# Modulation sums of a two-block transformer: when GpSimd sums over the partitions, and where the down products take their modulation units

## What is computed

```python
def mod_vectors(cvec, w_mod, b_mod):
    m = jax.nn.silu(cvec) @ w_mod + b_mod
    return jnp.split(m, N_MOD, axis=-1)

def sandwich_ffn(x, w_gate_up, w_down, g_pre, g_post, shift, scale, gate):
    h = modulate(rms_norm(x, g_pre), shift, scale)
    return x + 0.5 * gate * rms_norm(swiglu(h, w_gate_up, w_down), g_post)

for l in range(DEPTH):                       # DEPTH 2, N_MOD 9
    mx = [m[:, None, :] for m in mod_vectors(c, w_mod[l], b_mod[l])]
    mc = mod_vectors(c_ctx, w_mod[l], b_mod[l])
    ...
    x = sandwich_ffn(x, w_ffn_gate_up[l, 0], w_ffn_down[l, 0], g[0], g[1], mx[0], mx[1], mx[2])
    ctx = sandwich_ffn(ctx, w_ffn_gate_up[l, 0], w_ffn_down[l, 0], g[0], g[1], mc[0], mc[1], mc[2])
    ...
```

## Time and profile before

| | us |
|---|---|
| median of 3 runs | 2505.74 (2501.82 to 2506.13) |
| the profiled run | 2505.95 |
| its span, first to last instruction | 2504.1 |
| TensorE busy in it | 2429.5 (97%), 12978 matmuls |
| VectorE busy | 1545.5 (62%) |
| ScalarE busy | 1017.6 (41%) |
| GpSimd busy | 335.9 (13%) |

### The profile page before, as it was taken

How to read it: one execution, slowest core, us unless ns; L and a number is a source line. 1 busy time by engine, 2 the same in 40 slices (tenths; PEclk the granted TensorE clock), 3 DMA queues, 4 the chain that set the end, 5 groups by cost and what they waited for, 6 DMA issues and landing times.

```text
span 2504.1 us, 30960 instructions
## 1 busy us (share of the span) xinstructions
PE 2429.5 (97%) x12978; PEld 2056.5 (82%) x12978; DVE 1545.5 (62%) x2102; ACT 1017.6 (41%) x1429; POOL 335.9 (13%) x226
## 2 busy tenths in 40 slices
PE   7999999999999999999999999999999999999998
PEld 4887778857888778888888769987888899887997
DVE  6878796364778797444375565455466545586544
ACT  4221325375312225322225464345555434465443
POOL 0334242200143252101020200000000000000000
PEclk8999999989999999999999989999999999999999
DMA  7565552511465553444362625555534455533553
GB/s 283 184 170 183 171 177 93 156 35 65 154 185 173 165 181 121 152 137 153 115 219 76 147 68 189 180 179 178 184 119 152 135 186 185 160 129 117 190 182 142
DMA packets 242491, 386.04 MB, mean 154 GB/s; under 512 B 10864, under 2 KB 150256, under 8 KB 242288
## 3 DMA queue, kind: packets, MB, share of 16 engines
q1 hardware_dynamic: 236176, 372.43, 45.3%
q0 software_dynamic: 6176, 11.64, 2.5%
HBM read 382.83 MB, written 3.11 MB: 154 GB/s over the span
## 4 chain that ended last, share of the span: by engine, by line
PE 65%; DVE 17%; DMA 10%; ACT 4%; issue 3%; POOL 1%; SPq 0%; DVEq 0%; ACTq 0%; POOLq 0%
PE ps L532 20%; PE ps L533 20%; PE ps L534 20%; DVE arena L1871 8%; DMA raw<-in_w_mod 6%; DVE wlo L1848 4%; ACT whi L1231 2%; DVE arena L1868 2%; PE ps L602 1%; DMA raw<-in_w_ffn_down 1%; DMA arena<-rpbs 1%; PE ps L853 1%; DMA arena<-in_w_mod 1%; DMA raw<-in_w_ffn_gate_up 1%; DMA grow<-gcol 1%
## 5 line engine op out<-in xcount | busy, mean ns | idle before, releaser
L1848 DVE TENSOR_TENSOR wlo<-raw,whi 128x2048 fp32r<-128x2048 f32 x279 | 668.5, 2397 | 552.2 <-ACT whi L1231 551.9
L1231 ACT ACTIVATE whi<-raw 128x2048 fp32r<-128x2048 f32 x279 | 532.9, 1910 | 1131.3 <-PE ps L534 679.3
L532 PE MATMUL ps<-wlo,Hhi 128*128 128x512 f32 (+1 forms) x1888 | 707.9, 375 | 17.1 <-DVE Hlo L2057 10.8
L534 PE MATMUL ps<-whi,Hhi 128*128 128x512 f32 (+1 forms) x1888 | 697.5, 369 | 0.0
L533 PE MATMUL ps<-whi,Hlo 128*128 128x512 f32 (+1 forms) x1888 | 697.2, 369 | 0.0
L532 PE MATMUL ps<-Hlo,whi 128*128 128x512 f32 (+1 forms) x1896 | 639.7, 337 | 4.4 <-DVE wlo L1848 4.4
L533 PE MATMUL ps<-Hhi,wlo 128*128 128x512 f32 (+1 forms) x1896 | 638.6, 337 | 0.0
L534 PE MATMUL ps<-Hhi,whi 128*128 128x512 f32 (+1 forms) x1896 | 638.6, 337 | 0.0
L532 PEld LDWEIGHTS ps<-wlo,Hhi 128*128 128x128 f32 x1888 | 358.3, 190 | 85.0 <-DVE Hlo L2057 13.3
L534 PEld LDWEIGHTS ps<-whi,Hhi 128*128 128x128 f32 x1888 | 358.1, 190 | 60.1
L533 PEld LDWEIGHTS ps<-whi,Hlo 128*128 128x128 f32 x1888 | 358.6, 190 | 56.5
(11 more groups left out here) (262 smaller groups left out, 1584.3 us busy)
## 6 DMA issues: line engine op xcount, KB each, us to landing
raw<-in_w_ffn_gate_up SPq DMA_DIRECT2D x88, 1024.0 KB, 5.2
raw<-in_w_mod SPq DMA_DIRECT2D x65, 1024.0 KB, 5.1
raw<-in_w_ffn_down SPq DMA_DIRECT2D x44, 1024.0 KB, 4.9
raw<-in_ffn_w_in SPq DMA_DIRECT2D x44, 1024.0 KB, 5.0
raw<-in_attn_w_in SPq DMA_DIRECT2D x36, 1024.0 KB, 5.1
raw<-in_ffn_w_out SPq DMA_DIRECT2D x22, 1024.0 KB, 4.9
raw<-in_w_in SPq DMA_DIRECT2D x16, 1024.0 KB, 5.0
raw<-in_mlstm_w_in SPq DMA_DIRECT2D x12, 1024.0 KB, 5.1
```

What stands on the lines that cost most here:

```text
L532: e.matmul(o, L[0], R[1], start=start, stop=False)
L534: return e.matmul(o, L[0], R[0], start=False, stop=stop)
L1231: e.activation(hi_of(n), slot(n), ACT.Copy).then_inc(*A.up(("hi", n)))
L1848: e.tensor_tensor(lo_of(n), slot(n), hi_of(n).bitcast(F32), ALU.subtract).then_inc(*V.up(("lo", n)))
```

## The change

Three things change.

1. GpSimd waits for more before a sum. For a half (l, v, h) with stream s it used to wait for the half's own last multiply-add ("side") alone. Now, unless the half is the last of a group (`GROUP_ENDS`, h = 1), it waits for ("sum", next half, 4 s, 0) too: stream 0 for VectorE's first product of the next half, stream 1 for the first multiply-add of the next half's second unit. The semaphore is the same one, with a higher value.
2. A half is taken four ticks after its last unit, no longer three.
3. `SIDE_DOWN_AT` is range(8), no longer range(2, 8): the eight modulation units of a down net stand one behind each of its weight units 0 to 7. Before, units 2 and 5 had two behind them, and 3, 4, 6 and 7 one.

```diff
@@ Feed.tick
-        if self.summed and self.ticks - self.summed[0][1] >= 3:
+        if self.summed and self.ticks - self.summed[0][1] >= 4:
             yield from self.one()
@@
-SIDE_AT, SIDE_DOWN_AT = range(2, NF // 2 - 1), range(2, NF // 2 - 3)
+SIDE_AT, SIDE_DOWN_AT = range(2, NF // 2 - 1), range(NF // 2 - 3)
+GROUP_ENDS = [g[-1] for g in [*SIDE.values(), *SIDE_DOWN.values()]]
@@ summed_over_partitions
                     w.wait_ge(*V.at(("side", l, v, h)))
                     for s in range(ns):
+                        if (l, v) not in GROUP_ENDS or h == 0:
+                            w.wait_ge(*V.at(("sum", *acc_prev[q + 1], 4 * s, 0)))
                         t = SUMS[q % RING][s]
                         e.partition_all_reduce(t, t, 128, bass.bass_isa.ReduceOp.add).then_inc(
```

## The result

The changed kernel took 2519.31 us (median of 4 runs, 2518.57 to 2519.69) beside 2505.22 us before: a ratio of 1.0056, interval 1.004 to 1.0072, or +14 us. The prediction said 2511 us with a range to 2518. The direction was the likelier of its two by a hair, the size was nearly three times too small, and the time lies 1.3 us above the range.

What follows compares the result with a forecast made beforehand. TensorE, busy 2429.5 of 2504.1 us, bounds the kernel, with 18.9 us of pauses to win. Terms of +2.1 and +1.8 us, plus 1 us for thin margin, on 2505.95 gave 2511 us; range 2490 to 2518.

Steps and rivals of the forecast that it cites:

- The wait for the columns: VectorE's wait for pcol at a taking: stays about as it is, zero, bound 2 us per vector half.
- The clock: TensorE's granted clock behind new pauses: no loss in the forecast sum, falls of 1.7 us each only in a rival.
- the slot: Raw's slot for modulation units in gate_up: 24.5 us per pair, against 24.1 before and 21.76 needed by TensorE.
- The hold: VectorE inside the modulation unit: each sum holds up one multiply-add by 2.0 us, making it 2.7 us.
- The two rivals by which sums would wait or slip: Sums beside multiply-adds: all wait, 2489 or 2497 us, chance 0.22; one gets in, one waits, 2498 us, chance 0.13.
- the burst of small DMAs for the first gate vector: In the first gate_up: comes one step later, as its taking does, and costs the same.
- its own sign for this: VectorE's waits for pcol over 2 us per taking would break the term put at zero.
- the 5.4 foretold: First gate_up: TensorE goes on 5.4 us later, behind the wlo after the last two sums.
- the walk: VectorE's new order followed from 90 us with forecast durations: the first gate_up's last modulation unit ends at 270.3 us.
- L2107: Pause at the first down product, behind a modulation unit ahead of the last multiplies: 4.7 for 0.9 us, +3.8, twice.
- The Hlo waits: TensorE's waits in both downs: go with one unit per step, nearly all won, -7.1 and -7.2 us.
- The rival that held the clock: Pauses in the gate_ups bring four to six clock falls, 7 to 10 us: 2518 to 2521 us; shares chance 0.12.

Runs made afterwards that it cites:

- e7: The changed kernel with a threshold of five ticks in place of four: 2517.71 us, ratio 1.0058 against the kernel before.
- e5: The kernel before with parts 2 and 3, and the last multiplies of gate_up ahead of the modulation unit: 2484.56 us, ratio 0.9928.
- e1: The kernel before with only part 3, the spread of the down units: 2500.15 us, ratio 0.9989.
- T, D, W: On the kernel before, threshold of four (T), then spread of down units (D), then GpSimd's new waits (W): ratios 0.9964, 0.9962, 1.0056.
- e6: The changed kernel with the old places of the down units, so parts 1 and 2: 2528.33 us, ratio 1.0101 against the kernel before.
- Part 2 alone: The kernel before with only the threshold raised from three to four ticks: 2491.98 us, ratio 0.9964.
- e9: The changed kernel with the new wait on a half's first sum only, the second right behind it: 2514.40 us, ratio 1.0032 against the kernel before.
- e4: The kernel before with parts 2 and 3, without GpSimd's new waits: 2491.07 us, ratio 0.9962.
- e2: The kernel before with only GpSimd's new waits, threshold still three: 2614.15 us, ratio 1.0449.
- e11: The changed kernel with the last multiplies of gate_up ahead of the modulation unit: 2518.21 us, ratio 1.0052 against the kernel before.
- e12: The changed kernel with sums over only the first 256 of 512 columns, a measurement and no candidate: 2495.47 us (one run).

## Why the prediction was wrong

Three terms failed. The wait for the columns, put at zero with a bound of 2 us, was 5.4 us at one place where it counted. The clock, put at zero, took 5 us of the two downs. And the slot was sized a little small, 3.4 us in all. Then 5.4 us came back at places that the change doesn't touch, which is luck.

**The hold, right.** Each sum beside multiply-adds held one of them to 2.73 us, promptly. The two rivals by which sums would wait or slip are refuted by the 392 multiply-adds, whose mean rose from 754 to 951 ns. No multiply-add row stayed closed to a sum.

**The wait for the columns, put at zero, wrong.** The prediction wrote that "the wait for pcol stays about as it is" and that the burst of small DMAs for the first gate vector "costs the same". In total the waits for pcol did stay (14.7 us before, 13.5 after), but not in place. VectorE's longest one behind that burst was 1.7 us at 167 us before; in the changed kernel VectorE, and behind it ScalarE, have these rows:

```profile
184.15 0.17 DVE L1910 TENSOR_TENSOR mods<-pcol,vec 128x8 f32<-128x8 f32 x1 [5.44 <-DMA pcol<-prow]
188.79 0.23 ACT L1390 ACTIVATE arena<-arena 128x32 f32<-128x32 f32 x1 [1.96 <-DVE arena L2571]
188.93 1.89 ACT L1232 ACTIVATE whi<-raw 128x2048 fp32r<-128x2048 f32 x1
```

GpSimd was at the transfers of the gate vector until 167.0 us, so its sums and then the column came late. Behind the taking VectorE makes the tables for rope, for which ScalarE computes two sines (L1390), and only then does ScalarE cut the next weight unit. That unit, fetched at 171.40, had landed at 177.5. So whi, wlo (190.85), TensorE's pause of 4.3 us at 193 and the modulation unit from 193.06 to 200.4 all came 5.4 us later than they could. The prediction named its own sign for this, waits for pcol over 2 us per taking, and the sign came (5.4 here, 3.5 us at 970).

The first gate_up lost 11.5 us for the 5.4 foretold. Of the 6.1 between them 3.6 stand before 200.4 us: by the walk that unit ends at 196.8 (270.3 less three pairs of 24.5), and without the wait it would have ended at 195.0. e7, with no wait for pcol, had it end at 195.1 and the last unit at 270.4, as the walk had it; but other fetches were slow there, and its time was no better, so this share is read from the trace and not shown by a run.

**The slot, a little small.** 24.8 us per pair near 230 us for 24.5, and some pairs longer. The last three pairs took 75.2 us in either gate_up, for 73.5: 1.7 us each. That leaves 0.8 of the 6.1 behind the last unit. The second gate_up lost 8.0 us (18.6 less 10.6) for 5.2; of these 2.8 the slots are 1.7, and the other 1.1 was not taken apart.

**L2107, right.** 16.3 - 11.5 = 4.8 us and 22.7 - 18.6 = 4.1 us for 3.8 each. e5 shows that it is the modulation unit ahead of the multiplies.

**Down and the clock.** The Hlo waits went, in e1 as in the changed kernel. From the first down product to step 7 TensorE took 78.5 and 79.0 us. That is the 76.2 of the prediction and the 2.3 and 2.9 us of low clock behind the pauses of 5 us; the gain was 4.8 and 4.5 us for 7.1 and 7.2. So the clock, for which the sum held nothing, is a term of 5 us. The one pause of 3.0 us that the clock had survived was a weak witness for the pauses of 4 and 5 us that the prediction itself worked out. The rival that held the clock had a share of a chance of 0.12 and the time 2518 to 2521 us, which is where the kernel came out, but not by its sum: it charged four to six falls at 1.7 us each, and of the five that came three lie where TensorE is off the chain. Elsewhere the profiled run of before had low clock that the changed one had not. Two stretches behind pauses, before:

```profile
1704.00:1712.00 8.00, 7.91 (x32) 7.13 (x33) 2.71 (x5) 1.62 (x4) 0.00 (x0) 0.63 0.63 205
2229.00:2237.00 8.00, 8.00 (x28) 6.14 (x27) 7.11 (x25) 5.85 (x15) 0.00 (x0) 0.59 0.48 167
```

and the same places after:

```profile
1721.00:1729.00 8.00, 6.91 (x39) 5.91 (x40) 3.00 (x5) 3.46 (x4) 0.00 (x0) 1.00 0.66 205
2244.00:2252.00 8.00, 8.00 (x37) 6.50 (x37) 7.76 (x28) 5.84 (x16) 0.00 (x0) 0.79 0.48 157
```

That is 3.0 and 1.6 us, about the 4.5 us that came back between 970 us and the end, from no part of the change. The errors add up: 6.1 + 1.0 + 2.3 + 2.8 + 0.3 + 2.7 in the two pairs, less the 1 us set aside, 0.9 between the pairs and 4.5 behind them, is 8.8 us, as the span shows (13.7 for 4.9).

**The parts, wrong one by one.** The sum was made against before, in which a taking stood in the first hold, and in the changed kernel neither taking nor wlo stands in one. Part by part the prediction said +10.6, 0 and -6.7; in the order T, D, W the runs say -9.0, -0.5 and +23.5. Parts 1 and 2 together, without part 3, are +25 us (e6) for the prediction's 10.6, and part 3 behind them is -11. Part 2 alone is -9 us and part 1 alone, with a threshold of three, +112. A reader who dropped part 1 on the strength of the prediction would have looked for 2499 us and found 2491.

**What stays open.** In the changed kernel, e6 and e9, which pause by over 4 us at 193 us, whi starts 0.14 us behind the second sine, at 188.9, 189.3 and 188.7 us; in e4, without a pause, it does so too, but at 184.5. So the tables for rope stand ahead of that cut in all of them, and it matters how late VectorE comes to them. In e6 it waited 5.7 us for pcol, as in the changed kernel; in e9 only 1.5, and what made it late there was not taken apart. e2 has a pause of 6.3 us at 190.

## What to carry to other kernels

Price a move against the best place that the same work could have, not only against where it stands: here the sums had a better place already, behind the unit, where most of the hold meets instructions that it doesn't touch. When one tiny instruction reads ten times its length in the profile, ask for each part of the change whether it moves that instruction or the one that holds it. Over a slot that is slower than the engine it feeds, don't repair single pauses; shorten the slot (e7 and e11 moved pauses and gained nothing). And charge a fall of the clock only where TensorE is on the chain that sets the time.

## What the hardware showed that was not expected

- PARTITION_ALL_REDUCE of 128 x 512 runs 3.2 us and holds VectorE's instructions with two SBUF inputs for its first 2.1 us; one of 128 x 256, itself 1.87 us long, held a multiply-add for 0.84 us; those of 128 x 64, 0.66 us at the least and 1.0 on average, held none. A two-input instruction that reads PSUM (L2107) is not held; one of 8 elements per partition (L1928) is held like a large one, 2245 ns for 167.
- The clock behind pauses. The changed kernel and e1 to e12 have 34 pauses of TensorE of 3.8 to 8.0 us behind 100 us; over the 6 us behind every one the granted clock was 0.50 to 0.77. Of 122 shorter ones, 1.8 to 3.5 us (before's among them), 45 kept 1.00, up to one of 3.3 us, and the same pause kept it in one kernel and not in another. So, as an estimate from these and where TensorE itself sets the time, a pause of 4 us should be booked at 5.4 to 7 us, and one of 3 us may cost 3 or 6.
